# One decoder layer in fp32: operands of the seven products placed 32 bytes off, two decays by one product each, a few steps moved

## What is computed

```python
x = x + 0.5 * swiglu_ffn(x, ffn1_norm, ffn1_w_gate, ffn1_w_up, ffn1_w_down)
h = rms_norm(x, mix_norm)
gq, gk, gv, gz, ga, gb, mq, mk, mv, cq = split(h @ w_in)
y_gdn  = gated_deltanet(...)     # 4 heads x 128, chunked delta rule with decay
y_moba = moba_attention(...)     # 4 heads x 64, block-sparse, causal
y_mem  = memory_attention(...)   # 4 heads x 64, into 256 memory tokens
x = x + concat(y_gdn, y_moba, y_mem) @ w_out
x = x + 0.5 * swiglu_ffn(x, ffn2_norm, ffn2_w_gate, ffn2_w_up, ffn2_w_down)

def swiglu_ffn(x, gain, w_gate, w_up, w_down):
    h = rms_norm(x, gain)
    return (silu(h @ w_gate) * (h @ w_up)) @ w_down
```

## Time and profile before

| | us |
|---|---|
| median of 3 runs | 994.51 (994.26 to 994.87) |
| profiled execution | 994.35 |
| its span in the trace | 992.5 |
| TensorE busy | 987.5 (99%) |
| VectorE busy | 685.7 (69%) |
| GpSimd busy | 509.7 (51%) |
| ScalarE busy | 444.7 (45%) |
| loads | 26% of the 16 DMA engines |

### The profile page before, as it was taken

How to read it: one execution, slowest core, us unless ns; L and a number is a source line. 1 busy time by engine, 2 the same in 40 slices (tenths; PEclk the granted TensorE clock), 3 DMA queues, 4 the chain that set the end, 5 groups by cost and what they waited for, 6 DMA issues and landing times.

```text
span 992.5 us, 16521 instructions
## 1 busy us (share of the span) xinstructions
PE 987.5 (99%) x6833; PEld 872.2 (88%) x6833; DVE 685.7 (69%) x1092; ACT 444.7 (45%) x655; POOL 509.7 (51%) x297
## 2 busy tenths in 40 slices
PE   9999999999999999999999999999999999999998
PEld 7888999999999988788877888888999999999997
DVE  6894976676666497863547764789986676666745
ACT  8642444344443472534456764634343334433341
POOL 0355775676656433543252301645975666756741
PEclk9999999999999999999999999999999999999999
DMA  8432322332123312321221001322132333123312
GB/s 312 154 130 79 128 86 86 128 128 97 74 86 127 114 57 86 127 86 43 85 87 44 3 2 44 127 85 86 50 122 85 128 128 118 53 86 127 128 43 85
DMA packets 15914, 95.33 MB, mean 96 GB/s; under 512 B 2016, under 2 KB 2400, under 8 KB 5600
## 3 DMA queue, kind: packets, MB, share of 16 engines
q1 hardware_dynamic: 15696, 94.23, 26.4%
q10 hardware_dynamic: 144, 0.05, 0.0%
HBM read 92.17 MB, written 2.10 MB: 95 GB/s over the span
## 4 chain that ended last, share of the span: by engine, by line
PE 96%; DVE 3%; POOL 1%; issue 0%; ACT 0%; DVEq 0%; POOLq 0%
PE bank L2016 50%; PE bank L2142 35%; PE bank L2456 1%; PE bank L2542 1%; PE bank L2460 1%; PE bank L2482 1%; PE bank L2570 1%; PE bank L2559 1%; PE bank L2504 1%; PE bank L2194 1%; POOL wlo L517 0%; PE bank L2526 0%; DVE t_ffn_sum L1339 0%; PE bank L2606 0%; PE bank L2516 0%; PE bank L2628 0%
## 5 line engine op out<-in xcount | busy, mean ns | idle before, releaser
L2142 PE MATMUL bank<-t_ffn_hi,whi 128*128 128x256 f32 x952 | 269.4, 283 | 0.0
L2142 PE MATMUL bank<-t_ffn_hi,wlo 128*128 128x256 f32 x952 | 269.4, 283 | 0.0
L2142 PE MATMUL bank<-t_ffn_lo,whi 128*128 128x256 f32 x952 | 269.4, 283 | 0.0
L534 POOL TENSOR_TENSOR wlo<-sums,whi 128x512 fp32r<-128x512 f32 x136 | 184.7, 1380 | 131.8 <-ACT whi L739 131.7
L517 POOL TENSOR_TENSOR wlo<-raw,whi 128x1024 fp32r<-128x1024 f32 (+1 forms) x36 | 124.6, 3478 | 166.2 <-ACT whi L614 151.3
L534 POOL TENSOR_TENSOR wlo<-raw,whi 128x512 fp32r<-128x512 f32 x102 | 168.4, 1665 | 41.0 <-ACT whi L739 41.0
L2142 PEld LDWEIGHTS bank<-t_ffn_hi,whi 128*128 128x128 f32 x952 | 182.7, 192 | 0.7
L2142 PEld LDWEIGHTS bank<-t_ffn_lo,whi 128*128 128x128 f32 x952 | 182.7, 192 | 0.7
L2142 PEld LDWEIGHTS bank<-t_ffn_hi,wlo 128*128 128x128 f32 x952 | 182.7, 192 | 0.0
L2016 PE MATMUL bank<-ahi,whi 128*128 128x512 f32 x396 | 156.5, 395 | 0.4 <-POOL wlo L517 0.4
L2016 PE MATMUL bank<-ahi,wlo 128*128 128x512 f32 x396 | 154.4, 390 | 0.0
(11 more groups left out here) (339 smaller groups left out, 1405.1 us busy)
## 6 DMA issues: line engine op xcount, KB each, us to landing
raw<-fast_in SPq DMA_DIRECT2D x34, 1024.0 KB, 4.9
raw<-stream SPq DMA_DIRECT2D x26, 1024.0 KB, 4.9
raw_down<-fast_in SPq DMA_DIRECT2D x19, 1024.0 KB, 7.0
raw<-stream SPq DMA_DIRECT2D x7, 512.0 KB, 7.9
out<-x SPq DMA_DIRECT2D x7, 256.0 KB, 2.0
x<-x_in SPq DMA_DIRECT2D x3, 512.0 KB, 8.7
memx<-mem_in SPq DMA_DIRECT2D x2, 512.0 KB, 11.1
raw_gate<-stream SPq DMA_DIRECT2D x1, 1024.0 KB, 5.0
```

Of the source, the lines that this page charges most:

```text
L534: nc.gpsimd.tensor_tensor(in_ring(wlo, ring_at, n), whole[:, PIECE * at:PIECE * (at + 1)], in_ring(whi, ring_at, n).bitcast(F32), ALU.subt ...
L2142: ins = E.matmul(psum[bank][:, HALF * h:HALF * (h + 1)], a, b[:, k, :], start=start and k == 0 and m == 0, stop=k == K2 - 1 and m == 2, sk ...
```

## The change

- **Placement.** `SHIFT` is 32. The running address is moved up by 64 bytes ahead of `raw` and ahead of `ck`. So x, `ahi`, `alo`, `qkv`, `z`, `cq` and the products' other 512-wide operands stay at multiples of 256; `raw`, `whi`, `wlo`, `rbc`, `kt`, `pt`, `xt` and `at` are 64 bytes past one; all seven T of both FFNs are 32 bytes past one. A T then lies 32 bytes off the grid of the weights, a 512-wide operand 64 bytes off it, and before both were on it.
- **Decays of chunks 2 and 3.** `late_decays` makes each by one product of `picks` by `blocks`, as for chunks 0 and 1, both one behind the other ahead of `level_first(0, 6)`. For this `column_parts` moves within its buffer and the masks in `cst` are laid out anew (4 columns fewer to load). On TensorE `prep(2)`, `prep_scores(2)` and `prep_turn(2)` move forward past memory and score steps, and two banks are exchanged; on VectorE and ScalarE the steps around them are moved.
- **FFN2's first fast block.** VectorE's `ffn_add(before, 3)` stands ahead of `first_sums`.
- **The start.** `warm` is 128 x 128 instead of 128 x 512; 10 products on it instead of 11, each still 512 wide (the tile is read four times over). The high part of x's first piece is made by VectorE ahead of its first `wlo`, and no longer by ScalarE; ScalarE waits for it before its next. `first_pair` takes k = 0, 1 and 2 in the order that before k = 0 alone had.

The diff, cut to these:

```diff
+SHIFT = 32
...
+        cursor[0] += 2 * SHIFT
         raw, _, _ = place("raw", [P, RAW, 2048])
         whi, whi_at, _ = place("whi", [P, RING, 2048], F32R)
         wlo, wlo_at, _ = place("wlo", [P, RING, 2048], F32R)
...
-        column_parts, _, _ = place("column_parts", [P, 2, 16], F32R, at=columns_at)
+        column_parts, _, _ = place("column_parts", [P, 2, 16], F32R, at=columns_at + 64 * 4)
...
+        cursor[0] += 2 * SHIFT
         ck, _, _ = place("ck", [P, 2, M])
...
-        warm, _, _ = place("warm", [P, T], F32R, at=mid)
+        warm, _, _ = place("warm", [P, P], F32R, at=mid)
...
-        t_at = [[z_at, z_at + EIGHT, z_at + 2 * EIGHT, a_hi0, a_hi0 + EIGHT, a_lo0, a_lo0 + EIGHT],
-                [a_lo0, a_lo0 + EIGHT, cq_at, kt_at, kt_at + EIGHT, z_at, z_at + EIGHT]]
+        z_t, cq_t, a_hi_t, a_lo_t, kt_t = (at + SHIFT for at in (z_at, cq_at, a_hi0, a_lo0, kt_at - 2 * SHIFT))
+        t_at = [[z_t, z_t + EIGHT, z_t + 2 * EIGHT, a_hi_t, a_hi_t + EIGHT, a_lo_t, a_lo_t + EIGHT],
+                [a_lo_t, a_lo_t + EIGHT, cq_t, kt_t, kt_t + EIGHT, z_t, z_t + EIGHT]]
...
-                for d in range(PIECES[i], PIECES[i + 1]):
+                for d in range(max(PIECES[i], 1), PIECES[i + 1]):
+                    if d == 1:
+                        act.wait_ge(a_hi, 1)
                     x_high(0, S_G1, d)
...
+            dve.wait_ge(small_sem, 16)
+            dve.wait_ge(x_sem[0], 16)
+            V.tensor_scalar(x_hi[0][:, 0, :], x[:, 0, :], col(S_G1), None, ALU.mult).then_inc(a_hi, 1)
...
+                if f == 1:
+                    ffn_add(before, 3)
                 first_sums(f, 0, 1)
-                ffn_add(before, 3)
+                if f == 0:
+                    ffn_add(before, 3)
...
+            evacuate(25, z[:, 3, :])
             mem_max(6, 0)
...
-            evacuate(25, z[:, 3, :])
+            prep_decay(2)
             mem_scale(6, 0)
...
-            def prep_decay(c):
-
-                if c == 2:
-                    pe.wait_ge(mk_ready, 5)
-                else:
-                    pe.wait_ge(p_evac, 26)
-                for h in range(H):
-                    i = E.matmul(heads(PREP_BANKS[c][0])[:, h, :], gcol(G_G, h, c).broadcast_to([P, P]), upper,
-                                 start=True, stop=True)
-                    if c == 2 and h == 0:
-                        i.then_inc(w_used, 1)
-                i.then_inc(prep_ps[0], 1)
+            def late_decays():
+
+                pe.wait_ge(mk_ready, 5)
+                E.matmul(psum[PREP_BANKS[2][0]][:], picks[:, 2:3].broadcast_to([P, P]), blocks,
+                         start=True, stop=True).then_inc(w_used, 1)
+                pe.wait_ge(p_evac, 26)
+                E.matmul(psum[PREP_BANKS[3][0]][:], picks[:, 3:4].broadcast_to([P, P]), blocks,
+                         start=True, stop=True).then_inc(prep_ps[0], 2)
```

More of the change, by code:

```diff
@@ L1864, in _ @@
             mem_max(4, 1)
-            V.memset(xt[half[1], 0:2, :, half[0]], 0.0).then_inc(corner_zero, 1)
             mk_scale(0)
             mq_scale(0)
+            V.memset(xt[half[1], 0:2, :, half[0]], 0.0).then_inc(corner_zero, 1)
             level_update(0, 4)
@@ L1887, in _ @@
             mem_scale(6, 1)
-            prep_decay(2)
             prep_decay(3)
+            level_update(0, 6)
+            mem_out(5)
+            prep(2)
+            prep_scores(2)
             row_max(0, 0)
-            mem_out(5)
             row_max(0, 1)
-            prep(2)
-            level_update(0, 6)
-            prep_scores(2)
             prep_query(2)
@@ L2164, in first_pair @@
             def first_pair():
[L2166 to L2174, removed]
+                for k in range(3):
+                    low = (piece_lo, k + 1) if k < 2 else (w_lo, 1)
+                    pe.wait_ge(*((piece_hi, k + 1) if k < 2 else (w_hi, 1)))
+                    for (w, act_), (done, count) in zip(((whi, ahi), (wlo, ahi), (whi, alo)),
+                                                        ((a_hi, k + 1), low, (a_lo, k + 1))):
+                        pe.wait_ge(done, count)
+                        for bank in range(4):
+                            E.matmul(psum[bank][:], wslice(w, 0, k, bank * P, P, PAIR), act_[:, k, :],
+                                     start=k == 0 and w is whi and act_ is ahi, stop=False)
+                for k in range(3, KD):
                     pe.wait_ge(a_hi, k + 1)
@@ L2192, in ffn @@
                     pe.wait_ge(warm_ready, 1)
-                    for _ in range(11):
-                        E.matmul(psum[4][:], warm[:, 0:P], warm[:], start=True, stop=True)
+                    for _ in range(10):
+                        E.matmul(heads(4), warm[:], warm[:].unsqueeze(1).broadcast_to([P, H, P]), start=True, stop=True)
                     first_pair()
@@ L2409, in prep_scores @@
                 qb = PREP_BANKS[c][2]
-                if c == 3:
+                if c == 2:
+                    pe.wait_ge(y_sb, 3 * LAST)
+                elif c == 3:
                     pe.wait_ge(qe_ready, 3)
@@ L2735, in _ @@
             mem_turn(5)
-            prep_decay(3)
             prep(2)
+            level_second(0, 6)
+            mem_out(5)
+            prep_scores(2)
+            mem_turn(6)
+            prep_turn(2)
             scores(0)
-            mem_out(5)
-            level_second(0, 6)
-            mem_turn(6)
-            prep_scores(2)
             mem_out(6)
-            prep_turn(2)
             prep_turn_values(2)
@@ L2880, in constants @@
     r = np.where(i < 64, i % 16, -64)[:, None]
+    decay = np.where((i >= 64) & (i < 96), i % 16, -64)[:, None]
     keys = (i // 16 % 2 == 1)[:, None]
     n = np.arange(4)[None, :]
-    c[:, C_BLK:C_BLK + 4] = r // NC_ == n
-    c[:, C_BLK + 4:C_BLK + 8] = (r >= 0) & (r % 8 // 2 == n)
-    c[:, C_PICK:C_PICK + 4] = (r >= 0) & (r % NC_ == n)
+    c[:, C_BLK:C_BLK + 4] = ((r >= 0) & (r % 8 // 2 == n)) | (decay // NC_ == n)
+    c[:, C_PICK:C_PICK + 4] = (decay >= 0) & (decay % NC_ == n)
     pairs = (r // 8 == n // 2) & (r % 2 == n % 2)
```

18 lines of the change are left out of this document (9 added, 9 removed).

## The result

| | us | ratio to before |
|---|---|---|
| before, median (5 runs beside the changed kernel) | 994.51 | |
| changed, median of 5 runs (998.79 to 999.58) | 999.24 | 1.0049 (95% interval 1.0037 to 1.0061) |
| changed, span of the profiled execution | 997.4 | before: 992.5 |

A forecast was written before the change was run, and what follows sets the result against it. The prediction took TensorE's pitch of back-to-back products as the bound. It summed 994.35 - 9.4 (placement) - 1.4 (decays) - 0.3 (start) - 0.6 (FFN2) = 982.65 profiled, 982.8 us as median, range 969 to 994.5.

The forecast's parts named there:

- What bounds the kernel: TensorE's stream: its number or pitch of products decides, with 13.3 ns above the columns at both widths; the rest touches single microseconds.
- Placement of T: 2856 256-wide products, T 32 bytes off the weights' grid: pitch down 3.3 ns to 116.7 ns, -9.4 us, with small confidence.
- The 512-wide products: Operands on the grid, weights 64 bytes off: no change of pitch, with 1 ns (2.2 us) to either side.
- The slower one: Rival: reading T off the grid takes longer, +3.3 ns on T, 1001.6 us, up to 1004; chance 0.15.
- no effect: Rival: T stays at 120.0 ns and only the small parts count, 992.2 us, from 991.8 to 994.4; chance 0.27.
- The moved steps: Late decays, start and FFN2 edits together: -2.3 us, between -2.7 and -0.1.
- the start: TensorE's first real product, once VectorE makes the first high part: -0.3 us, between -0.5 and +0.4.
- The decays: Chunks 2 and 3: two 512-wide products replace two sets of eight records on TensorE, -1.4 us, between -1.5 and -0.6.
- FFN2's addition: VectorE's addition ahead of the weight sums closes TensorE's gap near 697 us: -0.6 us, between -0.6 and +0.1.
- the larger fall: Rival: placement removes most of the 13.3 ns, T at 111.3 ns, 967.4 us, from there up to 976; chance 0.2.
- the small parts: Decays, start and FFN2 beside the placement: -2.3 us together, stated bounds -2.7 and -0.1.

The follow-up runs named there:

- e1: The changed kernel with SHIFT 0: weights, T and 512-wide operands all on the 256-byte grid, every other edit kept; 992.15 us, ratio 0.9985.
- e2: The changed kernel with weights back on the 256-byte grid (gates tile moved ahead of raw), T still 32 bytes off; 984.93 us, ratio 0.9909.
- e4: The changed kernel with weights 64 bytes off the grid and T on it, distance 64 for both widths; 987.6 us in one run.
- e5: The changed kernel with weights on the grid, T 192 bytes off and the gates tile ahead of raw; 987.0 us, ratio 0.9926.
- e9: The changed kernel with weights on the grid, T 64 bytes off and the gates tile ahead of raw; 987.6 us in one run.
- e16: The changed kernel with x, its parts, the hidden parts and weights 64 bytes off, T on the grid, gates tile ahead of raw; 986.5 us, ratio 0.9924.
- e18: The changed kernel with weights 192 bytes off and T on the grid, timed again in five rounds; 980.34 us, ratio 0.9875.
- e12: The changed kernel with weights on the grid, T 32 off, FFN2's high part of x on the grid and VectorE's fourth addition behind the first weight sums; 983.71 us.
- e6: The changed kernel with weights 192 bytes off and T on the grid, the kernel of e18 in its first timing; 980.2 us in one run.
- e17: The changed kernel with T and the 512-wide operands 64 bytes off and weights on the grid, no gates tile ahead; 986.3 us in one run.
- e7: The changed kernel with weights 128 bytes off and T on the grid; 1001.6 us in one run.
- e10: The changed kernel with weights on the grid, T 128 bytes off and the gates tile ahead of raw; 994.8 us in one run.

## Why the prediction was wrong

**What bounds the kernel** was right: TensorE's pitch, and everything else touched single microseconds (-2.1 in e1). The forecast was 16.4 us too low: 4.8 of these are the term of T, 11.6 that of the 512-wide products.

**Placement of T** (-9.4). The reading that 13.3 ns are no floor was right. The size, 3.3 ns, came out for the place it was read at: `mv` has stationary operands on the grid and moving ones 32 past it, and e2, which is just that, has 116.7 ns. But that is luck. In `mv` k = 0, on the grid, has the same 120.0 ns as k = 1, so the rows show no effect of 32 bytes at all; the 3.3 ns came from comparing a 264-wide product with a 256-wide one. Nor does k = 5 stand out: starts are given to 0.01 us, so three products can't resolve less than 3.3 ns. The step that failed is the transfer to this change. Its weights went to 64, so T lies 32 *behind* them and not ahead. I wrote "32 bytes off" and dropped the sign; at that distance T is at 118.3, and the term is -4.6, not -9.4.

**The 512-wide products** ("I take nothing, with 1 ns to either side"): this is the step that made the forecast wrong, by 11.6 us. It took a 264-wide row for a 512-wide product, and misread it. k = 2 goes from 437.15 to 437.52, 123.3 ns each and not "nothing that stands out", though this too is within the rounding:

```profile
437.52 0.28 PE L2016 MATMUL bank<-whi,ahi 128*128 128x264 f32 x1
```

The runs show that the same distance has opposite effects on the two widths (e4: 113.4 and 233.1), so a row of one width says nothing about the other, and the bound of 1 ns had no row at all. The honest bound from the trace of before was that some 2240 products with no row at this distance might rise as far as the 256-wide were thought to fall. (Of the 2250 counted, 12 have 256 columns.)

**The rivals.** The slower one had the sum nearly right (1001.6) by another mechanism: T up by 3.3 ns. T went down. The rule of the Trainium skill in "SBUF — State Buffer", "Who interferes with whom", gave "no effect" for the placement. By that rule e1 and the changed kernel would be equal; they are 7 us apart, and the measurement decides: whatever ports there are, a placement isn't free. What the product of 256 columns costs above its columns is 6.7 to 13.4 ns here; the 2.5 ns that the Trainium skill has for a single product, in "TensorE: Matmul & The Clock Gate", "Back-to-back issue gap", are met nowhere.

**The moved steps**, by e1, whose trace has the order of the changed kernel and the pitches of before: the sum of -2.3 came as -2.1, in part by luck. The stretch of 168 products that began at 105.30 begins at 104.88 in e1, -0.4 for the start (forecast -0.3; where the clock rises late, 1.8 come back, outside the bound of +0.4). The decays gave 1.98 - 0.65 = -1.3 (forecast -1.4), and no wait of TensorE at `at` or `mem_prob` took their place. Another 0.5 us came from a wait that no term named, and that is gone in e1. Before, then e1, one product of the same stage:

```profile
525.71 0.50 PE L2578 MATMUL bank<-blocks,pairs_pick 128*128 128x512 f32 x1 [0.25 <-DVE mk L1680]
524.72 0.39 PE L2589 MATMUL bank<-blocks,pairs_pick 128*128 128x512 f32 x1
```

Which of the moved steps removed it was not tested. FFN2's addition gave nothing (forecast -0.6): the bound named there, that the sums end 0.7 later and the first product with no slack behind them gives it back, is what happened, on GpSimd's queue. The rows that follow FFN2's reordering say it: the block that begins at 784.00 in the chain of before begins at 781.68 in e1, as far ahead (2.32) as the start of FFN2 already was.

```profile
104.88 20.15 PE bank L2154 x168
...
604.10 50.56 PE bank L2028 x222
...
781.68 20.15 PE bank L2154 x168
```

(Before has 50.56 from 606.42 on: e1 is 2.32 ahead there too.)

**The range.** It was said to leave out the lower half of the larger fall and still took 0.15 of its 0.2; and the small parts' lower bounds add up to -2.6, not -2.7. Neither matters to the outcome.

**What stays open.** The pitch at a distance is read, not explained: why 64 apart helps at 256 columns and hurts at 512, and what sets the one of two pitches, apart from the one change seen at a short stall and the pattern with the wide products' distance. Kernels that by the distance would have T at 113.3 and the wide products at 226.7 (about 973 us by the sum) were tried three times, as e5, e9 and e16, and all had the slower pitch of T nearly throughout.

## To carry to other kernels

Where products stream back to back, the places of the moving operand and of the weights are a parameter to be swept, by distance modulo 256 with its sign and for each width of product apart; here it moved the changed kernel between 980.2 and 1003.6 us. A fixed part in the pitch that is the same for two widths needn't be a floor. And a pad that aligns one operand moves all that is allocated behind it: list the distance of every product, not only of those that are meant. Of the kernels tried, weights 192 bytes off and T on the grid (e18, 980.34 us) is the fastest in the median, with times up to 986.50; e12 (983.71, at most 984.76) has one pitch of T in all its blocks. And a forecast for a distance needs a row of the same width at the same signed distance, with enough products to outweigh the rounding.

## What the hardware showed that was not expected

The pitch of an otherwise equal stream of products with their own weights changes with the distance between the two operands: 256 columns between 113.3 and 120.1 ns, 512 columns between 226.7 and 233.3 ns, at the same granted clock of 1.0. In the traces at distances of 0 and 32 all stretches of 168 products of T had one pitch. At 64 T had one of two, 113.3 or 117.8 ns, within one execution (e5, e6, e17, e18) and in one stretch between two executions (e6 and e18); the wide products at -64 had 229.0 or 233.3. At 128 T had 118.7 and 120.1 in turn with the weights moved (e7), and 120.0 throughout with T moved (e10).
